# Two-layer hybrid decoder trunk on one core: last MLP product into the idle norm tiles, the second gap pair behind the fourth input unit, final gains on two engines, output by half rows

## The reference, cut to what matters

```
mod = silu(c) @ w_ada[l] + b_ada[l]                  # sh1, sc1, g1, sh2, sc2, g2
h = rms_norm(x, norm1_gain[l]) * (1 + sc1) + sh1
proj = h @ w_in[l]                                   # split among four head groups A, B, C, D
o = concat(differential, block-sparse, forgetting, indexer-selected attention)
x = x + g1 * (o @ w_out[l])
h = rms_norm(x, norm2_gain[l]) * (1 + sc2) + sh2
u = causal_conv_width_3(h @ w_ffn_up[l])             # 2 x 2816 channels
x = x + g2 * ((silu(gate(u)) * value(u)) @ w_ffn_down[l])
```

## Time and profile before

| | |
|---|---|
| median of three runs | 752.45 us |
| profiled execution, its own time | 749.67 us |
| its span, first to last instruction | 748.0 us |
| mean granted clock of TensorE | 0.986 |
| TensorE busy | 718.3 us (96%) |
| VectorE busy | 503.4 us (67%) |
| ScalarE busy | 394.3 us (53%) |
| GpSimd (POOL) busy | 125.9 us (17%) |
| moved by DMA | 158.35 MB, 212 GB/s in the mean |

### The profile page before, as it was taken

The page is one execution under the profiler, slowest core; times in us unless marked ns, Lnnn a source line. Parts: engine busy times, 40 slices in busy tenths (PEclk is TensorE's granted clock), DMA queues, the critical chain, the costliest instruction groups (busy, mean ns, idle before and its releaser), DMA issues.

```text
span 748.0 us, 14853 instructions
## 1 busy us (share of the span) xinstructions
PE 718.3 (96%) x6177; PEld 676.2 (90%) x6177; DVE 503.4 (67%) x896; ACT 394.3 (53%) x630; POOL 125.9 (17%) x91
## 2 busy tenths in 40 slices
PE   5879999999999999999999999999999999999995
PEld 4578888899999999999988987999899999999995
DVE  2355788645699788797757458963569666666664
ACT  2346754534575565646435775452466454445532
POOL 2000102204005555555010010220400000000001
PEclk9799999999999999999999999999999999999998
DMA  9999998738277868686944876574716555555501
GB/s 282 349 294 206 351 328 281 236 99 284 70 261 246 270 210 279 201 279 225 300 129 136 285 232 208 169 226 159 236 58 225 180 200 184 170 179 199 186 2 57
DMA packets 139543, 158.35 MB, mean 212 GB/s; under 512 B 4932, under 2 KB 133077, under 8 KB 139477
## 3 DMA queue, kind: packets, MB, share of 16 engines
q1 hardware_dynamic: 139476, 157.41, 66.1%
HBM read 155.76 MB, written 1.64 MB: 210 GB/s over the span
## 4 chain that ended last, share of the span: by engine, by line
PE 83%; ACT 5%; DVE 5%; issue 3%; SPq 2%; DMA 1%; POOL 0%; DVEq 0%; POOLq 0%; ACTq 0%
PE bank L887 23%; PE bank L889 22%; PE bank L888 22%; PE bank L901 4%; ACT w_hi L1302 2%; PE bank L1210 1%; DVE w_lo L1543 1%; PE bank L917 1%; PE bank L941 1%; ACT work L1458 1%; PE bank L1226 1%; PE bank L1225 1%; DMA direct<-in_w_ada 1%; PE bank L1103 1%; PE bank L1101 1%
## 5 line engine op out<-in xcount | busy, mean ns | idle before, releaser
L1543 DVE TENSOR_TENSOR w_lo<-raw,w_hi 128x2048 fp32r<-128x2048 f32 (+1 forms) x97 | 232.3, 2395 | 94.6 <-ACT w_hi L1302 94.4
L887 PE MATMUL bank<-act_hi,w_hi 128*128 128x256 f32 (+1 forms) x1008 | 289.0, 287 | 5.1 <-DVE act_lo L1558 4.4
L889 PE MATMUL bank<-act_hi,w_lo 128*128 128x256 f32 (+1 forms) x1008 | 285.2, 283 | 0.0
L888 PE MATMUL bank<-act_lo,w_hi 128*128 128x256 f32 (+1 forms) x1008 | 285.2, 283 | 0.0
L1302 ACT ACTIVATE w_hi<-raw 128x2048 fp32r<-128x2048 f32 (+1 forms) x97 | 182.8, 1888 | 145.3 <-PE bank L889 144.9
L887 PEld LDWEIGHTS bank<-act_hi,w_hi 128*128 128x128 f32 (+1 forms) x1008 | 192.5, 191 | 15.6 <-issue 14.3
L888 PEld LDWEIGHTS bank<-act_lo,w_hi 128*128 128x128 f32 (+1 forms) x1008 | 192.6, 191 | 0.1
L889 PEld LDWEIGHTS bank<-act_hi,w_lo 128*128 128x128 f32 (+1 forms) x1008 | 192.6, 191 | 0.0
L887 PE MATMUL bank<-mlp_hi,w_hi 128*128 128x256 f32 x384 | 109.1, 284 | 2.4 <-DVE mlp_lo L1852 2.4
L888 PE MATMUL bank<-mlp_lo,w_hi 128*128 128x256 f32 x384 | 108.7, 283 | 0.0
L889 PE MATMUL bank<-mlp_hi,w_lo 128*128 128x256 f32 x384 | 108.6, 283 | 0.0
(11 more groups left out here) (191 smaller groups left out, 857.4 us busy)
## 6 DMA issues: line engine op xcount, KB each, us to landing
direct<-in_w_ada SPq DMA_DIRECT2D x48, 1024.0 KB, 9.5
raw<-in_w_ffn_up SPq DMA_DIRECT2D x44, 1024.0 KB, 5.2
raw<-in_w_in SPq DMA_DIRECT2D x22, 1024.0 KB, 6.9
raw<-in_w_ffn_down SPq DMA_DIRECT2D x22, 1024.0 KB, 5.0
raw<-in_w_out SPq DMA_DIRECT2D x8, 1024.0 KB, 5.5
bias<-toeplitz SPq DMA_DIRECT2D x4, 384.0 KB, 11.8
heads_out<-in_x SPq DMA_DIRECT2D x1, 1024.0 KB, 5.4
out<-heads_out SPq DMA_DIRECT2D x2, 512.0 KB, 3.1
```

The lines of the kernel that those rows point to most:

```text
L887: pe.matmul(dst, lh, rh, start=first, stop=False, skip_group_check=check)
L888: pe.matmul(dst, lh, rl, start=False, stop=False, skip_group_check=check)
L889: return pe.matmul(dst, ll, rh, start=False, stop=last, skip_group_check=check)
L1543: nc.vector.tensor_tensor(w_lo[n % RAW][:, s], raw[n % RAW][:, s], w_hi[n % RAW][:, s].bitcast(F32), ALU.subtract).then_inc(lo_done, 1)
```

## The change

1. In the last step of each layer's MLP the product goes to `act_hi[:, 0:2]` and `act_lo[:, 0:2]`, and ScalarE's copy has no wait on the down product before it.
2. In layer 1 the second gap pair's turn and unit 3 change places with respect to the splits: split 4, unit 3, the turn, then split 5, the forget gate, and evacuation 3.
3. The final gains: VectorE makes tiles 0 to 3 after each residual, ScalarE tiles 4 and 5 between its squares, VectorE tiles 6 and 7 behind its last residual. TensorE's second group of transposes waits for the two semaphores.
4. The output is written in four writes of 256 KB, the first column half of both token tiles and then the second, each when its half is there.

```diff
@@ layer_schedule, l = 1 @@
         s += [("unit", 2, 4, KT), ("evac", 2), ("latents", 0)]
+        s += [("split_hi", 4), ("split_lo", 4)]
+        s += [("unit", 3, 0, KT)]
         s += [("pair_turn",) + p for p in gap[1:2]]
-        s += [("split_hi", 4), ("split_lo", 4)]
         s += [("split_hi", 5), ("split_lo", 5), ("forget", 0)]
-        s += [("unit", 3, 0, KT), ("evac", 3), ("latents_up", 0)]
+        s += [("evac", 3), ("latents_up", 0)]
@@ where a step's product goes @@
+        def gated(j):
+
+            return (act_hi[:, 0:2, :], act_lo[:, 0:2, :]) if j == STEPS - 1 else (mlp_hi[:, :, :], mlp_lo[:, :, :])
@@ SP @@
-            for t in range(TT):
-                sp.wait_ge(out_part[t], 2)
-                sp.dma_start(out[0, t * P:(t + 1) * P, :], x_tok[:, t, :]).then_inc(stored, 16)
-            sp.wait_ge(stored, 16 * TT)
+            for q in range(2):
+                for t in range(TT):
+                    sp.wait_ge(out_part[t], q + 1)
+                    sp.dma_start(out[0, t * P:(t + 1) * P, 512 * q:512 * q + 512],
+                                 x_tok[:, t, 512 * q:512 * q + 512]).then_inc(stored, 16)
+            sp.wait_ge(stored, 16 * 2 * TT)
@@ TensorE @@
+                    hi, lo = gated(j)
...
-                            mm = product3(down_part(ct), (wh[:, f, s], wl[:, f, s]), (mlp_hi[:, f, :], mlp_lo[:, f, :]),
+                            mm = product3(down_part(ct), (wh[:, f, s], wl[:, f, s]), (hi[:, f, :], lo[:, f, :]),
...
-                pe.wait_ge(fin_ready, 4 * (q + 1))
+                if q:
+                    pe.wait_ge(fin_act, 2)
+                    pe.wait_ge(fin_last, 2)
+                else:
+                    pe.wait_ge(fin_early, 4)
@@ ScalarE @@
-                    if j > 0:
+                    if 0 < j < STEPS - 1:
 
                         act.wait_ge(unit_used, first + 3 * j + 2)
-                    nc.scalar.activation(mlp_hi[:, :, :], prod, ACT.Copy).then_inc(mlp_hi_ready, 1)
+                    nc.scalar.activation(gated(j)[0], prod, ACT.Copy).then_inc(mlp_hi_ready, 1)
...
-            squares_of(2 * DEPTH)
+            for k in range(KT):
+                square(2 * DEPTH, k)
+                if k in (4, 5):
+                    nc.scalar.activation(final[:, k, :], xT[:, k, :], ACT.Identity,
+                                         scale=vec[:, 0, V_FIN + k:V_FIN + k + 1]).then_inc(fin_act, 1)
@@ VectorE @@
+            def with_gain(k, done):
+
+                dve.wait_ge(x_new, KT * 2 * DEPTH + k + 1)
+                nc.vector.tensor_scalar(final[:, k, :], xT[:, k, :], vec[:, 0, V_FIN + k:V_FIN + k + 1], None,
+                                        ALU.mult).then_inc(done, 1)
...
-                    nc.vector.tensor_tensor(mlp_lo[:, :, :], prod, mlp_hi[:, :, :].bitcast(F32),
+                    nc.vector.tensor_tensor(gated(j)[1], prod, gated(j)[0].bitcast(F32),
                                             ALU.subtract).then_inc(mlp_lo_ready, 1)
...
                     residual(l, 5, k, down_part(k))
-                    if l + 1 == DEPTH:
-
-                        dve.wait_ge(x_new, KT * 2 * DEPTH + k + 1)
-                        nc.vector.tensor_scalar(final[:, k, :], xT[:, k, :], vec[:, 0, V_FIN + k:V_FIN + k + 1], None,
-                                                ALU.mult).then_inc(fin_ready, 1)
+                    if l + 1 == DEPTH and k < 4:
+                        with_gain(k, fin_early)
...
+            for k in (KT - 2, KT - 1):
+                with_gain(k, fin_last)
             take_mean(2 * DEPTH)
```

More of the change, by code:

```diff
@@ L515, in trunk @@
         mlp_lo_ready = sem("mlp_lo_ready")
-        fin_ready = sem("fin_ready")
+        fin_early = sem("fin_early")
+        fin_act = sem("fin_act")
+        fin_last = sem("fin_last")
         stored = sem("stored")
```

## The result

The changed kernel takes 746.03 us (median of four executions, 745.57 to 746.99) against 752.39 for the kernel before; the ratio is 0.9919, with a 95% interval of 0.9902 to 0.9936.

A forecast was written before the change was run, and what follows sets the result against it. TensorE was taken to bound four fifths of the chain of waits. Terms 1.83 + 0.93 + 0.95 + 0.37 + 0.55 = 4.63 us took the profile from 749.67 to 745.0, 747.8 us in the timed median; range 746.3 to 750.8.

The forecast's parts named there:

- A: Last MLP step: product into act_hi and act_lo skips wait on down product 9; 1.83 us (layer 1), 0.93 (layer 0).
- the seam of 1.02: Layer 0, last down product: four column sums on TensorE's path take 1.02 us to the second matmul.
- B: Layer 1 input stage: second gap pair behind unit 3 removes a TensorE stall; `latents_up` starts 0.95 us earlier.
- the seam in front of unit 3: Layer 1, TensorE: four latents' transposes and the seam before unit 3's second matmul cost 0.61 us.
- the pair's transposes: Layer 1, TensorE: the second gap pair's transposes, now behind unit 3, take 0.66 us.
- the hand-over from VectorE back to TensorE: Layer 1: `latents_up` newly waits for VectorE's reduce, with a hand-over of 0.15 us.
- The queue behind the new wait: Layer 1: VectorE and ScalarE work runs 1.4 us later, fitting old idle time with 0.1 to spare; rival's chance 0.13.
- D: Output: four writes start the stream 0.7 us before the second half is ready; 0.55 us gained.
- C: Tail: final gains split over VectorE and ScalarE make the last square ready earlier; 0.37 us gained.
- So 737.48 + 4 x 0.39 + 2 x 0.40 = 739.84 plus write-out, against 740.25 before: Tail, ScalarE: after residual 4, four squares and two gains end at 739.84, 0.37 us earlier.
- The 2.78: Whole kernel: profiled execution's distance under the timed median, carried over unchanged from 745.0 to give 747.8 us.
- the larger B or C, 1.5 more than forecast: Range's lower end: a larger gain in layer 1's input stage or the tail's final gains, giving 746.3 us.

The follow-up runs named there:

- Part A in layer 0, run alone: Only layer 0's last MLP product moved into act_hi and act_lo, against the kernel before: median 748.60 us, ratio 0.9968.

## Why the prediction was wrong

**A**: 1.83 in layer 1 and 0.93 in layer 0 forecast, the same measured. Right, with its mechanism and the seam of 1.02. **B**: 0.95 forecast, 1.12 measured and 1.1 in the times. Three small terms were each a little large: the seam in front of unit 3 (0.61 forecast, 0.55 measured), the pair's transposes (0.66, 0.60) and the hand-over from VectorE back to TensorE (0.15, 0.11). The queue behind the new wait behaved as worked out, with 0.2 us of cover instead of 0.1. **D**: 0.55 forecast, 0.57 measured; the four writes overlap. The advice of the Trainium skill (DMA: Bandwidth & Descriptors, Bandwidth), at least 1 MiB for one DMA, did not bite here: four of 256 KB ran at 381 GB/s, two of 512 KB at 401.

**C**: 0.37 forecast, 0.00 measured. The failed step is "So 737.48 + 4 x 0.39 + 2 x 0.40 = 739.84 plus write-out, against 740.25 before". It takes the last square for the releaser of the mean. The row at 738.37, 24 mean records in 2.74 us without idle time, was there to be read: TensorE was still working off earlier tiles when the last square was ready. I followed the data and not the queue. The last square did come nearer to the last down product, by 0.64 us, more than forecast, and it bought nothing.

The sum of the terms came to 4.63 where 4.45 were to be had: a good size. What put the median outside the range was another step, **"That execution lies 2.78 under the median of the timed runs, 752.45; the same difference gives 747.8 us there."** The 2.78 was taken for a constant. It is the difference of two clock histories: the profiled execution lost 1.4 us in one gap, the usual one of that kernel about 3.5 in all. The changed kernel's usual execution loses about 1.9 (745.8 less 743.9). Filled gaps showed that the large steps come from there: the spread of both kernels shrank to about 1.2 us and their difference became 4.3. So 4.3 to 4.45 of the 6.0 us (pooled medians, 751.8 less 745.8) are stalls taken off the path, and 1.6 or so are half clock that the changed kernel meets less. Which part brings this surplus is open. Part A in layer 0, run alone, gave 2.4 us more than its work in the median, more than the whole surplus; taken out of the changed kernel, it cost only 0.5 us in the median of six (746.34 against 745.8), less than its work. These gifts don't add. What is shown is that an edit ahead of the gap changed the amount. Why it does is not: filling the stall did not bring it.

The sign was there: the profiled execution (749.67) stood outside of the three timed ones (751.46 to 752.70), and in its trace the second gap's window stood at 0.50 (shown above). The range had no term for the clock. Its lower end was also loose in itself: "the larger B or C, 1.5 more than forecast" is neither B's 1.10 (2.05 less 0.95) nor C's 0.78 (1.15 less 0.37) nor both, 1.88.

## What to carry to other kernels

When a profiled execution lies outside the range of the timed ones, find out what the difference consists of before carrying it over: read the granted clock in windows, stretch by stretch, and forecast the part of the work and the part of the clock each for itself. Compare lowest with lowest and median with median; an edit whose gain differs between the two has changed how often something falls, not only how long the work is. With six executions a step of 1.5 us that no edit touched can make such a difference too. And before costing an earlier operand, look at whether the engine that uses it was waiting for it: a group of records with no idle time in front says that it was not.

## What the runs showed of the hardware that was not expected

- One program on one core had several times, 748.2 to 753.2 us, in steps that go with half-clock stretches in two gaps of some 7 us and in one place among dense products, at 46 to 50 us. The stretches recorded were 3.4 us long and cost 1.4 to 1.5 us in any of the three, or 6.8 us long (first gap alone) and cost 3.1 us. No profile of eighteen shows one in the like gap of layer 0, near 184 us.
- TensorE was recorded as busy all through these gaps (2.00 of 2.00 us in the windows) and its clock fell all the same; with four more dense products of 0.55 us in each gap the times stayed together in all but two of 29 executions; with one product they did not.
- Removing a stall of 0.85 us changed the median by 3.2 us, and filling that stall with a product changed it by nothing.
- Four output writes of 256 KB with rows of 2 KB ran at 381 GB/s against 401 for two of 512 KB with rows of 4 KB.
